# A depthwise convolution on TensorE in 32x32 blocks, two groups side by side

## The reference, cut to what matters

```python
glu_a, glu_g = jnp.split(z[..., A_Q + 2 * A_KV:], 2, axis=-1)
u = glu_a * jax.nn.sigmoid(glu_g)
...
u_ext = jnp.concatenate([conv_hist.astype(u.dtype), u], axis=1)
c = jax.nn.silu(layernorm(causal_dwconv(u_ext, cw, cb), lng, lnb))
```

## Time and profile before

| | us |
|---|---|
| median of 3 runs | 2675.09 |
| lowest and highest run | 2673.5, 2675.83 |
| the profiled execution | 2667.71 |
| its span, from the first to the last instruction | 2665.8 |
| PE busy | 2592.5 |
| DVE, ACT, POOL busy | 1729.4, 957.2, 1516.9 |
| the 160 convolution matmuls (L1155), 320 records, busy | 49.1 |

### The profile page before, as it was taken

The page is one execution under the profiler, slowest core; times in us unless marked ns, Lnnn a source line. Parts: engine busy times, 40 slices in busy tenths (PEclk is TensorE's granted clock), DMA queues, the critical chain, the costliest instruction groups (busy, mean ns, idle before and its releaser), DMA issues.

```text
span 2665.8 us, 44321 instructions
## 1 busy us (share of the span) xinstructions
PE 2592.5 (97%) x17441; PEld 2509.1 (94%) x17441; DVE 1729.4 (65%) x2301; ACT 957.2 (36%) x1830; POOL 1516.9 (57%) x1527
## 2 busy tenths in 40 slices
PE   7999999999999999999999999989999999999997
PEld 7998789999999999999989898978999999999997
DVE  5216955766668777787546464654776666877776
ACT  4112643433334443442413323142433333434334
POOL 6542523777778887862322321343476666888873
PEclk9999989999999999999999999999999999999998
DMA  6321021333346433432133241433133334644332
GB/s 197 68 60 42 2 106 50 133 148 146 141 150 236 143 140 136 147 119 67 37 108 34 76 85 56 97 115 127 58 141 141 142 141 163 227 138 147 136 131 93
DMA packets 162942, 308.23 MB, mean 116 GB/s; under 512 B 61756, under 2 KB 77116, under 8 KB 161968
## 3 DMA queue, kind: packets, MB, share of 16 engines
q1 hardware_dynamic: 87808, 243.19, 27.0%
q10 hardware_dynamic: 74656, 61.22, 7.9%
q0 software_dynamic: 272, 0.98, 0.1%
HBM read 204.18 MB, written 95.85 MB: 113 GB/s over the span
## 4 chain that ended last, share of the span: by engine, by line
PE 83%; DVE 8%; DMA 2%; issue 2%; ACT 2%; POOL 2%; ACTq 0%; SPq 0%; DVEq 0%; POOLq 0%
PE psum L1028 46%; PE psum L973 20%; PE psum L1392 5%; PE psum L1155 2%; PE psum L1434 1%; PE psum L1000 1%; PE psum L1468 1%; PE psum L1474 1%; PE psum L1424 1%; PE psum L1236 1%; DVE low L1796 1%; PE psum L1277 1%; DMA out_qk_s<-high 1%; DVE low L2135 1%; DVE a_lo L1635 1%
## 5 line engine op out<-in xcount | busy, mean ns | idle before, releaser
L763 POOL TENSOR_TENSOR w_lo<-w_raw,w_hi 128x256 fp32r<-128x256 f32 (+1 forms) x478 | 438.9, 930 | 243.1 <-ACT w_hi L2355 243.0
L1028 PE MATMUL psum<-a_hi,w_hi 128*128 128x288 f32 x2032 | 434.6, 295 | 2.4 <-DVE low L1796 1.3
L1028 PE MATMUL psum<-a_lo,w_hi 128*128 128x288 f32 x2032 | 433.2, 295 | 0.0
L1028 PE MATMUL psum<-a_hi,w_lo 128*128 128x288 f32 x2032 | 433.2, 295 | 0.0
L1796 DVE TENSOR_TENSOR low<-low,psum 128x576 f32<-128x576 f32 x441 | 330.5, 750 | 153.8 <-PE psum L1028 151.3
L2355 ACT ACTIVATE w_hi<-w_raw 128x256 fp32r<-128x256 f32 (+1 forms) x478 | 210.3, 456 | 528.5 <-POOL w_raw L777 356.7
L1028 PE MATMUL psum<-op_h,w_hi 128*128 128x288 f32 x2040 | 354.1, 296 | 6.7 <-DVE low L1796 6.4
L1028 PEld LDWEIGHTS psum<-a_hi,w_hi 128*128 128x128 f32 x2032 | 326.0, 188 | 4.4 <-DVE low L1796 2.9
L1028 PEld LDWEIGHTS psum<-a_hi,w_lo 128*128 128x128 f32 x2032 | 326.3, 188 | 0.0
L1028 PEld LDWEIGHTS psum<-a_lo,w_hi 128*128 128x128 f32 x2032 | 326.3, 188 | 0.0
L973 PE MATMUL psum<-a_hi,w_hi 128*128 128x384 f32 x1272 | 303.2, 346 | 23.2 <-DVE a_lo L1581 17.1
(11 more groups left out here) (316 smaller groups left out, 4628.6 us busy)
## 6 DMA issues: line engine op xcount, KB each, us to landing
w_raw<-in_wall SPq DMA_DIRECT2D x159, 512.0 KB, 4.6
ffn_rows<-low SPq DMA_DIRECT2D x224, 288.0 KB, 2.2
mid<-ffn_rows SPq DMA_DIRECT2D x50, 576.0 KB, 3.7
rbc<-ffn_rows SPq DMA_DIRECT2D x48, 576.0 KB, 3.7
mid<-in_wall SPq DMA_DIRECT2D x32, 512.0 KB, 4.6
low<-in_x ACTq DMA_DIRECT2D x16, 576.0 KB, 8.9
high<-in_mem_in ACTq DMA_DIRECT2D x32, 257.0 KB, 4.2
out_mem_s<-high ACTq DMA_DIRECT2D x32, 257.0 KB, 3.3
```

The source lines that it names most:

```text
L763: nc.gpsimd.tensor_tensor(w_lo_flat[:, at], src, w_hi_flat[:, at].bitcast(F32), ALU.subtract)\
L1028: r = mm(psum[:, bank + i, 0:QT], v[:, at.start + P * k:at.start + P * (k + 1)], rows(part, k)[:, qtok(i)], start=start and k == 0 and n == 0,
```

## The change

Weights of a group are cut into four blocks of 32 rows and 32 columns, four channels each (`QC`); only the blocks on the diagonal are kept, side by side in 32 columns, so `build` writes 160 elements on each partition where it wrote 640, and needs a mask of 4 columns, which VectorE reduces from the one of 16. `conv(m)` now does a pair of groups: for each shift, for each of the two groups d, four matmuls, each of one block. Group d writes bank 6 + d; its block of rows 32i goes to partitions 32 ((i + d) mod 4), so group 1 comes out turned by 32 partitions. Pair m waits until ScalarE has read pair m - 1. The first pair of a burst runs inside the unit, ahead of its fifth k tile; the second behind the unit.

ScalarE reads a pair over both banks. Groups with d = 1 go back into channel order in two DMAs for one, 12 for each channel tile where there were 8. The calls at L2602 stand in another order: both reads of a tile's first burst come ahead of the next tile's `spread`, and the bias of the tile before stands between this `spread` and the second burst's reads.

```diff
-PH, GC = 8, 16
+PH, GC, QC = 8, 16, 4
 NG = P // GC
+CONV_OUTS = NG + NG // 2
...
-        toep = take(RING, REACH, P)
+        toep = take(RING, REACH, QC * PH)
...
-        same = take(GC)
+        same16 = take(GC)
+        same = take(QC)
...
                 if n == 0:
                     pool.wait_ge(taps_in, 16 * PH)
+                    pool.wait_ge(pads, 2)
                 if n >= RING:
                     pool.wait_ge(conv_sum, n - RING + 1)
-                full = [P, REACH, GC, PH]
+                full = [P, REACH, QC, PH]
...
-            def conv(n):
-
-                j, g = divmod(n, NG)
-                bank, at = 6 + n % BURST // 2, 256 * (n % 2)
-                if n == 0:
+            def conv(m):
+
+                j, g = divmod(2 * m, NG)
+                if m == 0:
                     pe.wait_ge(aux_read, AX_KROPE)
                 if g == 0:
                     pe.wait_ge(u_in[j], 16 * NG)
-                pe.wait_ge(toep_done, n + 1)
-                if n >= BURST:
-                    pe.wait_ge(conv_read, n // 2 - 1)
+                pe.wait_ge(toep_done, 2 * m + 2)
+                if m:
+                    pe.wait_ge(conv_read, m)
                 for a in range(REACH):
-                    r = mm(psum[:, bank, at:at + YCOL], toep[:, n % RING, REACH - 1 - a, :], uy[:, j % 2, g, a:a + YCOL],
-                           start=a == 0, stop=a == REACH - 1)
-                r.then_inc(conv_sum, 1)
+                    for d in range(2):
+                        for i in range(GC // QC):
+                            rows_, to = slice(32 * i, 32 * i + 32), 32 * ((i + d) % 4)
+                            r = mm(psum[to:to + 32, 6 + d, 0:YCOL], toep[rows_, (2 * m + d) % RING, REACH - 1 - a, :],
+                                   uy[rows_, j % 2, g + d, a:a + YCOL], start=a == 0, stop=a == REACH - 1,
+                                   tile_position=(32 * i, to), skip_group_check=True)
+                r.then_inc(conv_sum, 2)
...
                 def ready(k):
+                    if 0 <= u - FIRST_BURST < CT * NG // BURST and k == KT // 2:
+                        conv(2 * (u - FIRST_BURST))
...
                 if 0 <= b < CT * NG // BURST:
-                    for n in range(BURST * b, BURST * (b + 1)):
-                        conv(n)
+                    conv(2 * b + 1)
...
-            V.tensor_reduce(same, ident.rearrange("p (c f) -> p c f", f=PH), AX, ALU.add).then_inc(pads, 1)
+            V.tensor_reduce(same16, ident.rearrange("p (c f) -> p c f", f=PH), AX, ALU.add).then_inc(pads, 1)
+            dve.wait_ge(pads, 1)
+            V.tensor_reduce(same, same16.rearrange("p (i c) -> p c i", c=QC), AX, ALU.add).then_inc(pads, 1)
...
-                    src = psum[:, 6 + m % 2, :].rearrange("p (h n) -> p h n", h=2)
+                    src = psum[:, 6:8, 0:UCOL]
...
-                    for g in range(NG):
+                    for g in range(0, NG, 2):
                         dma(ud[GC * g:GC * (g + 1), j, :, 0:NM], uy[:, j % 2, g, 0:NM]).then_inc(conv_in[j], 16)
+                    for g in range(1, NG, 2):
+                        own, turned = GC * g, QC * PH
+                        dma(ud[own:own + 3 * QC, j, :, 0:NM], uy[turned:P, j % 2, g, 0:NM]).then_inc(conv_in[j], 16)
+                        dma(ud[own + 3 * QC:own + GC, j, :, 0:NM], uy[0:turned, j % 2, g, 0:NM]).then_inc(conv_in[j], 16)
...
             spread(0)
-            spread(1)
-            gather(0)
-            gather(1)
-            for j in (2, 3):
-                spread(j)
-                gather(2 * j - 2)
-                conv_bias(j - 2)
-                gather(2 * j - 1)
-            gather(6)
-            conv_bias(2)
-            gather(7)
-            conv_bias(3)
+            for j in range(CT):
+                gather(2 * j)
+                if j + 1 < CT:
+                    spread(j + 1)
+                if j:
+                    conv_bias(j - 1)
+                gather(2 * j + 1)
+            conv_bias(CT - 1)
```

More of the change, by code:

```diff
@@ L56 @@
 MN = NM // NT
-TOEP = REACH * P
 RING = 5
@@ L2566, in spread @@
                 act.wait_ge(u_done, j + 1)
-                act.wait_ge(pads, 2)
+                act.wait_ge(pads, 3)
                 act.wait_ge(hist_set, CT)
                 if j >= 2:
-                    act.wait_ge(conv_in[j - 2], 16 * NG)
+                    act.wait_ge(conv_in[j - 2], 16 * CONV_OUTS)
                 for g in range(NG):
@@ L2593, in gather @@
                     act.wait_ge(conv_read, BURST // 2 * (b + 1))
-                    for g in range(NG):
+                    for g in range(0, NG, 2):
                         dma(ud[GC * g:GC * (g + 1), j, :, 0:NM], uy[:, j % 2, g, 0:NM]).then_inc(conv_in[j], 16)
+                    for g in range(1, NG, 2):
+                        own, turned = GC * g, QC * PH
+                        dma(ud[own:own + 3 * QC, j, :, 0:NM], uy[turned:P, j % 2, g, 0:NM]).then_inc(conv_in[j], 16)
+                        dma(ud[own + 3 * QC:own + GC, j, :, 0:NM], uy[0:turned, j % 2, g, 0:NM]).then_inc(conv_in[j], 16)
             def conv_bias(j):
-                act.wait_ge(conv_in[j], 16 * NG)
+                act.wait_ge(conv_in[j], 16 * CONV_OUTS)
                 A(ud[:, j, :, 0:NM], ud[:, j, :, 0:NM], ACT.Identity, bias=cols[:, C_CB + j:C_CB + j + 1])\
@@ L2712, in sample_in @@
                 s = b % NCS
-                act.wait_ge(conv_in[s], 16 * CS_USES * h + (16 * (b // NCS) + 16 * NG))
+                act.wait_ge(conv_in[s], 16 * CS_USES * h + (16 * (b // NCS) + 16 * CONV_OUTS))
                 dma(csl[:, s, :], t["mem_in"][h, b]).then_inc(u_in[s], 16)
@@ L2887, in _ @@
             for s in range(NCS):
-                act.wait_ge(conv_in[s], 16 * CS_USES * MH + 16 * NG)
+                act.wait_ge(conv_in[s], 16 * CS_USES * MH + 16 * CONV_OUTS)
             act.wait_ge(cp_out, 16 * MH + ONE)
```

## The result

| | before | after |
|---|---|---|
| median, us | 2675.09 (3 runs), 2674.3 with a run beside those of after | 2651.97 (4 runs, 2649.96 to 2655.76) |
| ratio after / before | | 0.9921, 95% interval 0.9907 to 0.9935 |
| the profiled execution, us | 2667.71 | 2655.76 |
| its span, us | 2665.8 | 2653.9 |
| mean granted clock of that execution | 0.992 | 0.991 |

One execution of before, 3179.5 us at a mean granted clock of 0.75, was in a slower state and is left out of every comparison.

What follows compares the result with a forecast made beforehand. PE's own stream was taken to bound the kernel; convolution falls from 47.8 to 31.2 us, 16.6 saved, less a 0.6 us stall, so 16.0 us off the median 2675.09 gives 2659.1 us, range 2654 to 2672.

Steps and rivals of the forecast that it cites:

- What bounds the kernel: Units 3 to 10: PE's own stream sets the pace; eight convolution bursts, 47.8 us, are all the change can shorten.
- Eight blocks abreast: Convolution: eight 32x32 blocks run at once, 1.95 us a pair, 31.2 us for 16 pairs, 16.6 us saved on PE.
- Rivals 1 and 2: Convolution pairs: only four blocks abreast, 2680 us, chance 0.12; or instructions too slow, 2664 to 2674 (0.14), at worst 2741 (0.04).
- the far row of 85 ns: Instruction supply judged from 24 one-column matmuls with loads: 0.085 us each, 7.1 us a pair, 2741 us, chance 0.04.
- Two blocks abreast: Convolution, if row tiles queue for one PSUM bank: 6.2 us a pair, 52 us lost, 2727 us.
- ScalarE's one buffer: Each convolution pair fills both banks and waits for ScalarE's read of the one before: 0.6 us stall, bounds 0 and 3.1.
- The term of 0.6 us: PE's stall for ScalarE's late reads in the convolution stage, taken off the 16.6 us saved.
- The bound of 3.1 us: Upper bound of PE's stall for ScalarE's reads: up to 1.5 us twice and 0.2 us once.
- What costs nothing: Earlier first pair, twelve DMAs for eight, the last tile's bias and VectorE's added reduction were to cost PE no time.
- The sum: 16.6 - 0.6 = 16.0 us off PE's path, subtracted from the median 2675.09: 2659.1 us, forecast chance 0.63.
- the low end of the range: 2654 us for the whole kernel, taking 19 us saved and the scatter of the median.

Runs made afterwards that it cites:

- after again: The changed kernel itself, unaltered, run again for a second profile and more times: 2651.29 us, ratio 0.9906.

## Why the prediction missed

**What bounds the kernel.** Right: PE's stream was the stage, and it still is.

**Eight blocks abreast.** Right, and shown by taking the turn away (3.12 us) and by the order of issue (2.56, 4.42 us). The price was mis-sized a little: 1.87 us a pair for 1.95, so 17.9 us off 16 pairs and not 16.6. Streaming with rounds of 150 ns is 1.50 us; stagger and change-overs together are 0.37 us where 0.47 was put down.

**Rivals 1 and 2.** Neither came. Eight records on eight places start within 0.06 us (records on a restricted table of stretches, after again; PE's are the first count):

```profile
66.01:66.07 0.06, 0.05 (x8) 0.06 (x12) 1.00 0.00 0
```

Four row bands write one bank at once there, to different partitions. The rule of the Trainium skill ("TensorEngine Tiling (Array Packing)", Gotcha 1) that different row tiles cannot access one PSUM bank at the same time does not hold in this form. Nor does the floor of about 25 ns from matmul to matmul that the Trainium skill gives ("TensorE: Matmul & The Clock Gate", Wait — 56ns, not 53.3ns?) hold across places: starts are 6.7 ns apart within a round, 18.7 on the mean. What reads as a limit of supply came at 12.6 ns a record with its load (88 columns), and the far row of 85 ns was no measure of it. (Two blocks abreast would have lost 51 us by the prediction's own terms, 16 x 6.17 - 47.8, not 52.)

**ScalarE's one buffer.** The term of 0.6 us was 0: the chain came out at 11.90 us instead of 13.27, a shortening of 1.4 us where "1.1 us or more" stood, and the read is 0.5 us ahead. The bound of 3.1 us counted waits alone. Waits of 0.5 and 0.7 us cost no more than some 0.1 us beyond themselves, but 5.8 us of waiting cost 8.5, by the clock; what 1.5 us would have cost no run shows.

**What costs nothing.** Right: the start half a unit earlier, twelve DMAs, the last bias and VectorE's reduction left no wait of PE in the stage.

**The sum, where it failed.** The forecast was 7 us too slow. The stage gave 18.0 to 18.4 us, not 16.0: 2 us of the miss, 1.3 from the pair and 0.6 from the stall that did not come. The other 5 lie in one step, "the gain is a difference in one stage, so I subtract it from the median": it put every other difference between the executions at nothing, and the low end of the range left some 2 us for them. The executions of before lie up to 14 us apart, and about half of that scatter goes with the granted clock. The median of three, 2675.09, stood 1.7 us above the mean of 52, the executions of after had 1.8 us from a higher mean clock, and 1.6 us are open: with 18.2 us off 2673.4 the forecast would have been 2655.2, and the last two lead to the 2651.8 measured.

The 7.4 us between the profiled execution and the median, which were not followed up, were 8.0 us of one stretch at 130.0 ns, to be read from the trace of before by counting records in 100 us. That would have confirmed the median as the base. Taken from the profiled execution, 16.0 us would have given 2651.7, the measured time by luck.

The eight executions of after lie between 0.991 and 0.995 themselves. Why they kept the higher clock a little longer on the mean is not settled; no run was made on it.

## To carry to other kernels

Small blocks pay if each of them has a place of its own in the array (rows and columns) and the order of issue goes round the places; the same 80 records took 1.65, 2.56, 3.12 or 4.42 us by place and order alone. A buffer that is halved costs nothing as long as it is read before its next use: here half a unit of other work did that with 0.5 us to spare, with both pairs in a row it cost 4.6 us, and with the reader's work in another order the whole gain. A long wait of PE costs clock too (0.7 us cost hardly more than itself, 5.8 us cost 8.5). Before a gain is subtracted from a time, the spread of that time has to be traced to its stretches, by pace and by granted clock.

## What the hardware showed unexpectedly

- Products of 288 columns ran a whole stretch of 2400 records at 130.0 ns from start to start in one execution, and at 133.3 ns in the same stretch of the others, at clock 1.00 in both; what chose the pace is not known.
- PE starts records of another place ahead of waiting ones. In both seams seen the new place began when three records for each old one were waiting.
- Records on different places start 6.7 ns apart as long as a store of some 32 of them lasts; behind it most neighbours are 16.7 ns apart on sixteen places (176 columns), and 12.6 on the mean on eight (88 columns).
- The granted clock fell to 0.50 towards the end of waits of PE of 5.8 us. It also fell in a stage where PE never waited but had two places of sixteen at work for 4.4 us in each half unit (0.75 on the mean from 75 to 91 us).
